# One matmul of 512 columns for the high weight half, with the parts added when a projection is drained

## Chip, cores and metric

One core of a Trainium2 chip runs one program that holds a whole small network. The metric is the device time of one execution in microseconds, lower is better; the median of several executions is compared. TensorE (PE) multiplies, ScalarE (ACT) and VectorE (DVE) work on the results and prepare operands, GpSimd (POOL) and SyncE (SP) only issue transfers here, apart from small things.

## What is computed

256 tokens of width 2048 pass through two blocks, in float32. The first has two layers, each an RMS norm, a wide input projection (`w_in`), three attention mixers behind it, an output projection (`w_o`), and a gated addition with a second projection:

```python
for i in range(DEPTH):
    u = rms_norm(h, norm_g[i])
    z = u @ w_in[i]
    ...
    h = h + mixed @ w_o[i]
    h = h + (p[i] @ w_ple[i]) * jax.nn.sigmoid(h @ w_pg[i])
```

The second block has four layers on `x` and on a context of 256 tokens: Fourier mixing, window attention, a gated depthwise convolution, Fourier mixing. Each begins with a modulated norm and ends with a gated addition, and shift, scale and gate come from a product of a condition vector with the modulation weights:

```python
shift, scale, gate = ada_modulation(c, ada_w[i], ada_b[i])   # silu(c) @ w + b, 2048 x 6144 a layer
h = rms_norm_2(x, norm_g[i]) * (1.0 + scale[:, None, :]) + shift[:, None, :]
...
x = x + gate[:, None, :] * o
```

## The kernel before

**Splits.** TensorE multiplies in fp32r, a reduced format. Full precision is kept by splitting each operand into a high and a low half: weights into `whi` (an ACT cast, L1092, the helper `split` on ACT) and `wlo` (a DVE subtraction, L1701, `split` on DVE), activations into `uhi` and `ulo`. A product is the sum of three: `whi`*`uhi` (L529), `whi`*`ulo` (L530), `wlo`*`uhi` (L533).

**Slabs and groups.** Weights stream from HBM in slabs of 128 x 2048 floats (1 MB), four buffers of them (`raw`, with `wlo` in the same place; `whi` has two). A group is four slabs (s = 0 to 3) and gives four blocks of 128 output channels x 256 tokens, which fill two PSUM banks. Slab s holds input tiles kt = 4s to 4s+3 for all four blocks, so `slab_t` issues 16 pairs L529/L530, and then 16 times L533. Groups take the bank pairs 0/1 and 2/3 in turn, so that a group's drain may last as long as the next group's four slabs. `stream_plan` lists the runs: `in0`, `in1` (the input projections), `ga` (gates), `ple`, `o`, `pg`, and in the second block `fci`, `fco`, `fxi`, `fxo`, `f3i`, `f3o` (Fourier in and out on context, x, and the last layer), `kvc`, `kvx`, `qz`, `ao` (attention), `ci`, `co` (convolution). Kind "T" are those that go through `slab_t`. In the before kernel that includes `ga`.

**Order.** On ACT and DVE every run is an order written by hand: `run` calls the splits, two slabs ahead of TensorE, the drain of group g-1 after the split of slab 1 of group g, hooks (squares and folds of the next norm), and on DVE `ada(r, pos)`. A drain either copies (`copier`, ACT), applies a function into a buffer (`gater`, ACT), or adds to the residual with a gate (`adder`, DVE).

**Modulation pieces.** The modulation product is not on TensorE: 384 pieces of 128 x 1024 floats (0.5 MB) are loaded by POOL (L473) into two buffers `aslab`, and each is one multiply-and-sum on DVE (L1726), or two for the first 160 pieces, which serve both conditions. `ada_due` says how many pieces are taken at each slab position of each run.

**Borders.** Where a run needs a norm of what the run before it made, the norm stands between them (`norm`: n0, n1, nci, nf3, end), or is made in chunks while the last group runs (`norm_chunks`: nfc, nfx, nkc, nx1). In `norm` the sum of squares goes over TensorE (L652), and then DVE and ACT make `uhi`/`ulo` tile by tile, and TensorE waits for each tile of slab 0. After tile 8 DVE puts the split of slab 1 in between.

Of the kernel before, what the change touches and what calls it, by code (L numbers as in the profile page):

```python
# [17 lines left out]
F32 = mybir.dt.float32  # L18
# [50 lines left out]
def stream_plan():  # L69
# [32 lines left out]
    m = a = e = 0  # L102
    for r in runs:
        r["m0"], r["a0"], r["e0"] = m, a, e
        m += r["n"]
        a += r["ada"]
        e += r["steps"]
# [7 lines left out]

def ada_due(r, pos):

    def upto(p):
        if r["name"] in ("in0", "in1"):
            return 30 * min(max(p - 3, 0), 25) // 25  # L120
        if r["name"] == "ci":
            return min(p, r["ada"])
        if r["name"] in ("ga0", "ga1", "pg1", "fco", "fxo"):
            return r["ada"] * min(p, 13) // 13
        if r["name"] == "fci":
            return 14 * min(p, 16) // 16 + max(0, p - 16)
# [6 lines left out]
        if r["name"] == "o1":  # L133
            return min(p, 3) + 10 * max(0, p - 7) // 9
# [22 lines left out]
TAIL_NORMS = ("n0", "n1", "nx1", "nci", "nf3", "end")  # L157
U_NORMS = {n: i for i, n in enumerate(n for n in FILLS if n[0] == "n")}
# [35 lines left out]
def build(nc, w, vec, out):  # L194
    ctx = ExitStack()
    with ctx:
# [20 lines left out]
        uhi_t = sb("uhi", KT * T, F32R)  # L217
        ulo_t = sb("ulo", KT * T, F32R)
# [80 lines left out]
        bank = [ctx.enter_context(nc.psum_tensor(f"bank{i}", [P, 512], F32)) for i in range(8)]  # L299
# [27 lines left out]
        s_drain = sem("projection_drained")  # L327
        s_gu = sem("gate_used")
# [50 lines left out]
        s_cg = sem("conv_gates_ready")  # L379
# [20 lines left out]
        def squares(name, c):  # L400
# [3 lines left out]
            return (sq[:, 0:1024], sq[:, 1024:2048], pt[:, :], sq[:, 1024:2048])[c]  # L404

# [61 lines left out]
        def _(pool):  # L467
# [30 lines left out]
            for i, b in enumerate(PE_BLOCKS):  # L498
# [3 lines left out]
                pool.wait_ge(s_drain, 2 * (RUN["ci"]["e0"] + b // 2 + 1))  # L502
# [10 lines left out]
        def _(pe):  # L513
# [11 lines left out]
            def step_banks(e):  # L525
                return (bank[2 * (e % 2)], bank[2 * (e % 2) + 1])
# [8 lines left out]
            def slab_t(s, par, lows, ready=None):  # L535
                for k in range(4):
                    kt = 4 * s + k
                    if ready is not None:
                        pe.wait_ge(*ready(kt))
# [59 lines left out]
            def group(r, g, par, slab, fill=None, after=None, middle=None):  # L599

                e = g + r["e0"]
                if not (isinstance(e, int) and e < 2):
                    pe.wait_ge(s_drain, (e - 1) * 2)
                for s in range(SLABS):
                    if fill in NORMS and slab is slab_t:
                        pe.wait_ge(s_hi, (g + r["m0"]) * SLABS + (s + 1))
                        slab(s, par, False, lambda kt: (s_nl, 16 * U_NORMS[fill] + kt + 1))
# [13 lines left out]
            def project(name, fill, g0=0, n=None, sums=()):  # L621
# [4 lines left out]
                if sums:  # L626
                    for g in range(g0, g0 + n):
# [4 lines left out]
                        group(r, g, (r["e0"] + g) % 2, slab, fill if g == g0 else None, behind)  # L632
                    return
                for g in range(g0, g0 + min(n, 2)):
                    group(r, g, (r["e0"] + g) % 2, slab, fill if g == g0 else None)
                if n > 2:
                    with pe.Fori(g0 // 2 + 1, (g0 + n) // 2) as j:
                        for half in range(2):
                            group(r, j * 2 + half, (r["e0"] + half) % 2, slab)
                    if n % 2:  # L640
                        group(r, g0 + n - 1, (r["e0"] + n - 1) % 2, slab)

            def norm(name):
# [6 lines left out]
                if tail:  # L650
                    pe.wait_ge(s_sf, 4 * n + 4)
                    last = nc.tensor.matmul(bank[7][:, 0:T], ones[:, :], squares(name, 3)[:, 0:T],  # L652
# [11 lines left out]
            def first_block(l):  # L664
# [34 lines left out]
                for g in range(3):  # L699
                    group(r, g, (r["e0"] + g) % 2,  # L700
# [90 lines left out]
                for g in range(4):  # L791
                    group(r, g, (r["e0"] + g) % 2, slab_t, None, lambda s, g=g: point(2 * (4 * g + s) + 1),
# [4 lines left out]
                for s in range(SLABS):  # L797
                    pe.wait_ge(s_drain, 2 * (r["e0"] + s - 1))
                    pe.wait_ge(s_lo, SLABS * r["m0"] + s + 1)
                    b0, b1 = step_banks(r["e0"] + s)  # L800
# [11 lines left out]
            def up(l, jobs):  # L812
# [12 lines left out]
                for b in range(15):  # L825
                    e = r["e0"] + b // 4
                    o = step_banks(e)[(b % 4) // 2][:, T * (b % 2):T * (b % 2) + T]
# [4 lines left out]
                    if b % 4 == 0:  # L832
                        pe.wait_ge(s_drain, 2 * (e - 1))
# [14 lines left out]
                for part, (s, c0, n) in enumerate(((2, 1024, 512), (3, 0, 256))):  # L848
                    e = r["e0"] + 4 + part
                    pe.wait_ge(s_drain, 2 * (e - 1))  # L850
                    need(s)
                    for t in range(2):
                        tk = slice(P * t, P * (t + 1))
                        o = step_banks(e)[t][:, 0:n]
# [10 lines left out]
            def fourier(tag, n_inv):  # L865
# [50 lines left out]
                for g in range(4, 8):  # L916
                    group(r, g, (r["e0"] + g) % 2, slab_t, None, lambda s, g=g: after(4 * (g - 4) + s))
# [22 lines left out]
            for g in range(4, 8):  # L940
                group(r, g, (r["e0"] + g) % 2, slab_t, None, lambda s, g=g: rope_behind(4 * (g - 4) + s))
            pe.wait_ge(s_ro, 2 * NJ + NJX)

            U0, T0 = 2 * N1, 2 * NT1
# [1780 lines left out]
```

## Time and profile before

| | us |
|---|---|
| runs before (3) | 3159.17 to 3162.21, median 3160.34 |
| the profiled execution | 3164.51 |
| its span, first to last instruction | 3162.8 |
| PE busy | 2995.5 (95%) |
| DVE busy | 2435.8 (77%) |
| ACT busy | 1364.2 (43%) |
| mean granted TensorE clock | 0.981 |

Busy time of an engine is time in which at least one of its instructions runs. Matmuls overlap in the records, so the distance between the starts of two of them, not the duration of one, says what a matmul costs in a stream. The three runs and the profiled execution lie within 0.17%.

### The profile page before, as it was taken

To read this page: it belongs to the slowest core of one execution; us is meant where nothing else is said; L and a number is where in the kernel's file an instruction comes from. 1 tells how busy PE (TensorE), PEld (TensorE's weight loads), DVE (VectorE), ACT (ScalarE), POOL (GpSimd) and SP (SyncE) were. 2 spreads that over 40 slices of the span, in tenths; PEclk is the share of its full clock that TensorE was granted. 3 is DMA by queue.
4 is the path that set the end of the run, shared out by engine and by line. 5 is a ranking of instruction groups with operands and counts; after the bars stand their busy time and mean duration, and the time that the engine had idled before them with its cause. 6 is when DMAs were issued, how large, how long until landed. Compare 5 with 4: busy or idle time off the path is not lost.

```text
span 3162.8 us, 57851 instructions
## 1 busy us (share of the span) xinstructions
PE 2995.5 (95%) x23922; PEld 2868.5 (91%) x23922; DVE 2435.8 (77%) x3378; ACT 1364.2 (43%) x1480; POOL 274.4 (9%) x530
## 2 busy tenths in 40 slices
PE   5999999989999999999999998999898999989998
PEld 5997889989978899899999998998698999889998
DVE  7877888888888889975875777677878976577465
ACT  4444553343444644443443444334734333534343
POOL 0100000101000000000000110100010422000000
PEclk9999999989999999999999999999999999999999
DMA  6875547758845487675767774865276765477563
GB/s 230 294 268 173 169 160 265 256 200 290 287 160 174 161 295 278 214 258 202 280 236 256 258 276 163 301 242 192 81 254 212 228 197 195 152 261 249 204 227 133
DMA packets 130956, 706.32 MB, mean 223 GB/s; under 512 B 16393, under 2 KB 16545, under 8 KB 72609
## 3 DMA queue, kind: packets, MB, share of 16 engines
q1 hardware_dynamic: 67392, 480.28, 43.5%
q0 software_dynamic: 61264, 214.93, 20.0%
q10 hardware_dynamic: 2064, 7.70, 0.7%
q8 instruction: 182, 2.98, 0.4%
q14 instruction: 54, 0.43, 0.0%
HBM read 696.07 MB, written 2.10 MB: 221 GB/s over the span
## 4 chain that ended last, share of the span: by engine, by line
PE 59%; DVE 11%; issue 3%; ACT 3%; DMA 2%; DVEq 0%; POOLq 0%; ACTq 0%
PE bank L533 18%; PE bank L529 16%; PE bank L530 16%; DVE wlo L1701 3%; DMA aslab<-w_ada_dram 2%; DVE aslab L1726 2%; ACT whi L1092 2%; PE bank L881 1%; DVE sc L1872 1%; PE bank L995 1%; DVE junk L1726 1%; PE bank L661 1%; PE bank L902 1%; PE bank L953 1%; DVE yc L2456 1%
## 5 line engine op out<-in xcount | busy, mean ns | idle before, releaser
L529 PE MATMUL bank<-uhi,whi 128*128 128x256 f32 x6656 | 1651.6, 288 | 54.2 <-ACT whi L1092 18.1
L530 PE MATMUL bank<-ulo,whi 128*128 128x256 f32 x6656 | 1635.0, 285 | 0.0
L1092 ACT CAST whi<-raw 128x2048 fp32r<-128x2048 f32 x456 | 861.1, 1890 | 1424.6 <-PE bank L533 1386.4
L1701 DVE TENSOR_TENSOR wlo<-raw,whi 128x2048 fp32r<-128x2048 f32 x456 | 1034.7, 2270 | 440.7 <-ACT whi L1092 440.1
L529 PEld LDWEIGHTS bank<-uhi,whi 128*128 128x128 f32 x6656 | 1293.3, 194 | 66.9 <-issue 48.2
L530 PEld LDWEIGHTS bank<-ulo,whi 128*128 128x128 f32 x6656 | 1293.3, 194 | 3.0 <-issue 2.4
L533 PE MATMUL bank<-uhi,wlo 128*128 128x256 f32 x6656 | 880.6, 285 | 22.9 <-DVE wlo L1701 22.8
L533 PEld LDWEIGHTS bank<-uhi,wlo 128*128 128x128 f32 x6656 | 834.7, 193 | 28.8 <-DVE wlo L1701 26.1
L473 POOL DMA_DIRECT2D aslab<-w_ada_dram x384 | 203.7, 531 | 2636.0 <-DVE mod L1726 1392.3
L1726 DVE CUSTOM_DVE_ANT_0 aslab<-aslab,sil,part 128x1024 f32<-128x1024 f32 x192 | 245.1, 1280 | 47.5 <-DMA aslab<-w_ada_dram 47.5
L1726 DVE CUSTOM_DVE_ANT_0 aslab<-aslab,sil,cols 128x1024 f32<-128x1024 f32 x192 | 245.3, 1280 | 46.5 <-DMA aslab<-w_ada_dram 46.5
L1726 DVE CUSTOM_DVE_ANT_0 junk<-aslab,sil,cols 128x1024 bf16<-128x1024 f32 x80 | 102.4, 1280 | 23.3 <-DMA aslab<-w_ada_dram 20.2
L1726 DVE CUSTOM_DVE_ANT_0 junk<-aslab,sil,part 128x1024 bf16<-128x1024 f32 x80 | 102.3, 1279 | 9.7 <-DMA aslab<-w_ada_dram 7.5
L2456 DVE SCALAR_TENSOR_TENSOR yc<-gp,cols,yc 128x256 f32<-128x256 f32 x240 | 97.4, 478 | 0.0
L533 PE MATMUL bank<-whi,ulo 128*128 128x512 f32 (+2 forms) x256 | 84.5, 344 | 0.0
L594 PE MATMUL bank<-whi,uhi 128*128 128x512 f32 (+1 forms) x192 | 72.7, 391 | 1.1 <-ACT whi L1092 1.1
L1387 ACT ACTIVATE sc<-sc,sm 128x128 f32<-128x128 f32 x84 | 37.6, 448 | 64.1 <-DVE sm L2153 63.9
L1601 ACT ACTIVATE xs<-xs,sm 128x513 f32<-128x513 f32 x64 | 45.8, 717 | 30.7 <-DVE sm L2396 30.7
L533 PEld LDWEIGHTS bank<-whi,ulo 128*128 128x128 f32 x256 | 50.2, 196 | 8.1 <-issue 3.4
L1235 ACT ACTIVATE uhi<-sc,mod 128x256 fp32r<-128x256 f32 x64 | 29.2, 504 | 60.5 <-DVE sc L1872 57.7
L533 PE MATMUL bank<-wlo,uhi 128*128 128x512 f32 (+2 forms) x256 | 53.6, 336 | 0.0
L2396 DVE CUSTOM_DVE_ANT_0 xs<-bank,k,lamr 128x512 f32<-128x512 f32 x64 | 45.5, 748 | 8.9 <-PE bank L953 8.7
(289 smaller groups left out, 2283.7 us busy)
## 6 DMA issues: line engine op xcount, KB each, us to landing
aslab<-w_ada_dram POOLq DMA_DIRECT2D x384, 512.0 KB, 5.2
raw<-w_wfi_dram SPq DMA_DIRECT2D x96, 1024.0 KB, 5.1
raw<-w_win_dram SPq DMA_DIRECT2D x88, 1024.0 KB, 5.2
raw<-w_wfo_dram SPq DMA_DIRECT2D x48, 1024.0 KB, 5.1
raw<-w_wci_dram SPq DMA_DIRECT2D x48, 1024.0 KB, 5.2
raw<-w_wo_dram SPq DMA_DIRECT2D x32, 1024.0 KB, 6.2
raw<-w_wpg_dram SPq DMA_DIRECT2D x32, 1024.0 KB, 5.5
raw<-w_wqz_dram SPq DMA_DIRECT2D x32, 1024.0 KB, 5.1
```

What stands on the lines that cost most here:

```text
L473: pool.dma_start(aslab[:, slot, :], w["ada"][i]).then_inc(s_araw[slot], 16)
L529: nc.tensor.matmul(o, w_, xhi_, start=start, stop=False, skip_group_check=True)
L530: nc.tensor.matmul(o, w_, xlo_, start=False, stop=False, skip_group_check=True)
L533: return nc.tensor.matmul(o, w_, xhi_, start=False, stop=stop, skip_group_check=True)
L594: nc.tensor.matmul(o, uhi[:, kt, tk], whi[:, s % 2, wc], start=kt == 0, stop=False, skip_group_check=True)
L1092: nc.scalar.copy(whi[:, s % 2, 0:n], raw[:, s, 0:n]).then_inc(s_hi, 1)
L1387: last = nc.scalar.activation(x, x, ACT.Exp, bias=sm[:, SM_NM + c:SM_NM + c + 1], scale=-1.0, accum_out=sm[:, SM_SUM + c:SM_SUM + c + 1])
L1601: nc.scalar.activation(x, x, ACT.Exp, bias=sm[:, SM_NM + c:SM_NM + c + 1], scale=-1.0, accum_out=sm[:, SM_SUM + c:SM_SUM + c + 1]).then_in ...
L1701: v.tensor_tensor(wlo[:, s, 0:n], raw[:, s, 0:n], whi[:, s % 2, 0:n].bitcast(F32), ALU.subtract).then_inc(s_lo, 1)
L1726: ins = v.tensor_tensor_reduce(out=junk[:, :] if c else x, in0=x, in1=sil[:, c if both else 1 - half, :], scale=1.0, scalar=col("ada_b_2", ...
L2396: v.tensor_tensor_reduce(out=xs[:, 2 * (t % 3) + odd, 0:512], in0=bank[odd][:, :], in1=mask2[:, b], scale=-0.125, scalar=nsink[:, h:h + 1] ...
L2456: ins = v.scalar_tensor_tensor(out=yc[:, b, :], in0=x, scalar=wt, in1=yc[:, b, :], op0=ALU.mult, op1=ALU.add)
```

## The change

In the projections of kind "T" (all but `ga`, which gets its own kind "G" and the old slab layout) the two matmuls with `whi` become one: `uhi` and `ulo` now lie in one tensor, and the moving operand is both of them, 2 x 256 columns. A block then needs a whole PSUM bank: `whi`*`uhi` and `wlo`*`uhi` in columns 0 to 255, `whi`*`ulo` in columns 256 to 511. The slabs are laid out anew on the host: slab s holds eight input tiles for two of the four blocks, slabs 0 and 2 for the first two blocks, slabs 1 and 3 for the other two. The bank pairs change with each slab, so the first half of a group is complete after slab 2, the second after slab 3, and each half must be drained before the same slab parity of the next group begins.

The drain adds the parts: ACT copies the second part to SBUF (`corr`), DVE adds it to the first (`onto_copy`, or `in_place` in PSUM, after which ACT applies its function, `post`); `adder` does two rounds from PSUM. Drains go by halves and stand before the split of slab 0 and of slab 1 of the next group. The last squares before a border go by halves too, and a filled chunk of activations is now awaited by slab pairs (`chunk_free`). The modulation pieces are given out anew.

```diff
-        run(f"in{l}", "T", "win", 11 * l, 7, ada=30)
+        run(f"in{l}", "T", "win", 7 * l, 7, ada=26)
-        run(f"ga{l}", "T", "win", 11 * l + 7, 4, ada=13)
+        run(f"ga{l}", "G", "wga", 4 * l, 4, ada=(8, 13)[l])
-        run(f"o{l}", "T", "wo", 4 * l, 4, ada=(17, 13)[l])
-        run(f"pg{l}", "T", "wpg", 4 * l, 4, ada=(18, 14)[l])
+        run(f"o{l}", "T", "wo", 4 * l, 4, ada=(16, 13)[l])
+        run(f"pg{l}", "T", "wpg", 4 * l, 4, ada=(12, 8)[l])
...
-            run("qz", "T", "wqz", 0, 8, ada=36)
+            run("qz", "T", "wqz", 0, 8, ada=50)
-            run("ao", "T", "wao", 0, 4, ada=18)
+            run("ao", "T", "wao", 0, 4, ada=20)
-            run("co", "T", "wco", 0, 4, ada=18)
-        run(which + "i", "T", "wfi", 8 * j, 8, ada={"fc": 30, "fx": 42, "f3": 32}[which])
-        run(which + "o", "T", "wfo", 4 * j, 4, ada=0 if which == "f3" else 12)
+            run("co", "T", "wco", 0, 4, ada=16)
+        run(which + "i", "T", "wfi", 8 * j, 8, ada={"fc": 28, "fx": 54, "f3": 32}[which])
+        run(which + "o", "T", "wfo", 4 * j, 4, ada={"fc": 12, "fx": 14, "f3": 0}[which])
...
         if r["name"] == "qz":
-            return 20 * min(p, 16) // 16 + max(0, p - 16)
+            return 26 * min(p, 16) // 16 + 24 * max(0, p - 16) // 16
         if r["name"] == "fxi":
-            return 18 * min(p, 16) // 16 + 24 * max(0, p - 16) // 16
+            return 24 * min(p, 16) // 16 + 30 * max(0, p - 16) // 16
...
             def slab_t(s, par, lows, ready=None):
+                for k in range(8):
+                    kt = 8 * (s // 2) + k
+                    if ready is not None and ready(kt) is not None:
+                        pe.wait_ge(*ready(kt))
+                    for b in range(2):
+                        wc = slice(2 * P * k + P * b, 2 * P * k + P * (b + 1))
+                        o = bank[2 * par + b]
+                        if lows:
+                            last = low(o[:, 0:T], wlo[:, s, wc], uhi[:, kt, :], kt == KT - 1)
+                        else:
+                            last = nc.tensor.matmul(two(o[:, :]), whi[:, s % 2, wc], both_u[:, :, kt, :],
+                                                    start=kt == 0, stop=False, skip_group_check=True)
+                return last
...
+            def copier(dest):
+                def corr(r, g, half):
+                    second_parts(r, g, half)
+                    nc.scalar.copy(two(dest(g, half)), rest_of(r, half)).then_inc(s_cq, 1)
+                return corr, no_corr
...
+            def in_place(r, g, half, x):
+                dve.wait_ge(s_cq, SUMMED[r["name"], g, half][0])
+                half_summed(r, g, half)
+                v.tensor_tensor(main_of(r, half), main_of(r, half), x, ALU.add).then_inc(s_add, 1)
+
+            def onto_copy(r, g, half, x):
+                dve.wait_ge(s_cq, SUMMED[r["name"], g, half][0])
+                half_summed(r, g, half)
+                v.tensor_tensor(x, main_of(r, half), x, ALU.add).then_inc(s_drain, 1)
...
+                def add(r, g, half):
+                    at = 1024 * g + 512 * half
+                    half_summed(r, g, half)
+                    for part in range(2):
+                        src = (rest_of, main_of)[part](r, half)
```

## Rows read from the trace of the kernel before

**Rows 1.** The page's chain of work that ended last, shares of the span.

```profile
PE 59%; DVE 11%; issue 3%; ACT 3%; DMA 2%; DVEq 0%; POOLq 0%; ACTq 0%
```

**Rows 2.** Stretches: us, busy PE, PEld, DVE, ACT, POOL (count), PEclk, DMA share, GB/s.

```profile
546.00:649.00 103.00, 97.11 (x773) 96.70 (x772) 91.84 (x104) 40.61 (x30) 10.07 (x19) 0.95 0.76 264
...
1190.00:1282.00 92.00, 91.92 (x766) 91.69 (x765) 88.81 (x99) 43.90 (x32) 8.48 (x16) 1.00 0.78 274
...
1500.00:1593.00 93.00, 93.00 (x776) 92.95 (x775) 72.05 (x73) 40.85 (x28) 9.01 (x17) 1.00 0.77 277
...
1960.00:2060.00 100.00, 96.96 (x794) 96.58 (x794) 69.89 (x76) 42.66 (x38) 11.13 (x21) 0.98 0.79 277
```

**Rows 3.** The chain within 1500 to 1593 us, and within 2374 to 2500 us.

```profile
by line: PE bank L533 33.5%; PE bank L530 33.0%; PE bank L529 33.0%; PE bank L648 0.5%
by line: DVE wlo L1701 16.8%; DVE yc L2456 16.0%; issue 10.1%; DVE aslab L1726 9.8%; PE bank L529 7.6%; PE bank L530 7.4%; PE bank L533 7.1%; DMA aslab<-w_ada_dram 6.2%; DVE sc L1872 5.1%; DVE ulo L1883 4.1%; PE bank L995 2.9%; ACT whi L109
```

**Rows 4.** Groups of matmuls by shape: count, busy us, mean ns, idle before.

```profile
L529 PE MATMUL bank<-uhi,whi 128*128 128x256 f32 x6656 | 1651.6, 288 | 54.2 <-ACT whi L1092 18.1 <-DVE ulo L1883 10.6 <-DVE ulo L1880 8.5
L533 PE MATMUL bank<-uhi,wlo 128*128 128x256 f32 x6656 | 880.6, 285 | 22.9 <-DVE wlo L1701 22.8
L594 PE MATMUL bank<-whi,uhi 128*128 128x512 f32 x128 | 55.8, 436 | 1.1 <-ACT whi L1092 1.1
```

**Rows 5.** Timeline: start us, us; every second matmul of two steady streams.

```profile
200.23 0.28 PE L529 MATMUL bank<-uhi,whi 128*128 128x256 f32 x1
...
200.47 0.28 PE L529 MATMUL bank<-uhi,whi 128*128 128x256 f32 x1
...
214.13 0.39 PE L594 MATMUL bank<-whi,uhi 128*128 128x512 f32 x1
...
215.04 0.39 PE L594 MATMUL bank<-whi,uhi 128*128 128x512 f32 x1
```

**Rows 6.** Groups of DVE and ACT that drain or split: count, busy us, mean ns.

```profile
L1825 DVE TENSOR_TENSOR h<-bank,h 128x512 f32<-128x512 f32 x16 | 10.2, 681 | 0.0
L1830 DVE SCALAR_TENSOR_TENSOR h<-bank,mod,h 128x256 f32<-128x256 f32 x64 | 26.5, 475 | 14.7 <-PE bank L533 14.7
L1092 ACT CAST whi<-raw 128x2048 fp32r<-128x2048 f32 x456 | 861.1, 1890 | 1424.6 <-PE bank L533 1386.4 <-PE bank L523 26.2 <-PE bank L861 4.9
L1160 ACT ACTIVATE zq<-bank 128x512 f32<-128x512 f32 x16 | 8.6, 592 | 9.6 <-PE bank L533 9.6
```

**Rows 7.** Waits of PE within 546 to 700 us: total, times, longest.

```profile
PE bank L533 <- DVE wlo L1701: 10.1, 3, 4.3
```

**Rows 8.** Timeline of the border from `ao` over the norm nci to `ci`.

```profile
2391.91 1.66 DVE L1830 SCALAR_TENSOR_TENSOR h<-bank,mod,h 128x256 f32<-128x256 f32 x4 [4.92 <-PE bank L533]
2393.65 1.06 ACT L1187 ACTIVATE sq<-h 128x1024 f32<-128x1024 f32 x1 [4.02 <-issue]
2394.74 0.69 DVE L1778 TENSOR_TENSOR sq<-sq 128x512 f32<-128x512 f32 x1 [1.17 <-ACT sq L1187]
...
2402.49 0.55 PE L529 MATMUL bank<-uhi,whi 128*128 128x256 f32 x1 [5.32 <-DVE ulo L1883]
...
2407.94 2.08 PE L533 MATMUL bank<-uhi,wlo 128*128 128x256 f32 x16
...
2409.60 0.48 DVE L1883 SCALAR_TENSOR_TENSOR ulo<-sc,mod,uhi 128x256 fp32r<-128x256 f32 x1
```

**Rows 9.** Timeline of DVE and POOL in `qz`: a split, pieces, a load, a late piece.

```profile
1989.23 2.29 DVE L1701 TENSOR_TENSOR wlo<-raw,whi 128x2048 fp32r<-128x2048 f32 x1 [3.46 <-ACT whi L1092]
1991.44 1.28 DVE L1726 CUSTOM_DVE_ANT_0 aslab<-aslab,sil,part 128x1024 f32<-128x1024 f32 x1
...
1992.65 1.28 DVE L1726 CUSTOM_DVE_ANT_0 aslab<-aslab,sil,part 128x1024 f32<-128x1024 f32 x1
...
2001.27 0.53 POOL L473 DMA_DIRECT2D aslab<-w_ada_dram  x1 [6.16 <-DVE mod L1726]
...
2005.46 1.28 DVE L1726 CUSTOM_DVE_ANT_0 aslab<-aslab,sil,cols 128x1024 f32<-128x1024 f32 x1 [3.57 <-DMA aslab<-w_ada_dram]
```

More of the change, by code:

```diff
@@ L1138, in run @@
-                if (n - 1) % 2:
-                    body(g0 + n - 1, (r["e0"] + g0 + n - 2) % 2, fill)
+                g = g0 + n - 1
+                following = then if then is not None else (early,)
+                nxt, g1 = following[0], following[1] if len(following) > 1 else 0
+                corr(r, g, 0)
+                if nxt is not None:
+                    split(RUN[nxt], g1, 0)
+                post(r, g, 0)
+                hook(g + 1, 0)
+                corr(r, g, 1)
+                if then is not None:
+                    split(RUN[nxt], g1, 1)
@@ L1140, in run @@
+                post(r, g, 1)
                 if fill is not None:
-                    split(RUN[then[0]], 0, 0)
                     fill(2)
-                    split(RUN[then[0]], 0, 1)
-                elif then is not None:
-                    presplit(*then)
-                if early is not None:
-                    split(RUN[early], 0, 0)
-                drain(r, g0 + n - 1, (r["e0"] + g0 + n - 1) % 2)
-                if fill is not None:
-                    fill(3)
-            def nothing(r, g, par):
-                pass
@@ L1155, in copier, with run_one @@
-            def copier(dest, func=ACT.Copy):
-                def drain(r, g, par):
-                    summed(r, g)
-                    for half in range(2):
-                        last = nc.scalar.activation(dest(g, half), bank[2 * par + half][:, :], func)
-                    last.then_inc(s_drain, 2)
-                return drain
-            def gater(first, func, g0):
-                def drain(r, g, par):
+                    fill(3)
+            def run_one(r, drain, then):
+                split(r, 0, 2)
+                split(r, 0, 3)
+                presplit(*then)
+                drain(r)
@@ L1734, in run @@
                 n = r["n"] if n is None else n
+                add, use = drain
                 def hook(g, s):
@@ new lines, in copier, with applier, add, gater @@
+            def copier(dest):
+                def add(r, g, half):
+                    onto_copy(r, g, half, two(dest(g, half)))
+                return add, no_step
+            def applier(dest):
+                def add(r, g, half):
+                    in_place(r, g, half, two(dest(g, half)))
+                return add, no_step
+            def gater(first, g0):
+                def dest(g, half):
+                    at = 1024 * ((first + g - g0) % 2) + 512 * half
+                    return sq[:, at:at + 512]
+                return applier(dest)
@@ new lines, in adder, with add @@
+            def adder(dest_t, gate):
+                def add(r, g, half):
+                    at = 1024 * g + 512 * half
+                    half_summed(r, g, half)
+                    for part in range(2):
+                        src = (rest_of, main_of)[part](r, half)
+                        if gate is None:
+                            last = v.tensor_tensor(two(dest_t[:, at:at + 512]), src, two(dest_t[:, at:at + 512]),
+                                                   ALU.add)
+                        else:
+                            for b in range(2):
+                                y = dest_t[:, at + T * b:at + T * (b + 1)]
+                                last = v.scalar_tensor_tensor(out=y, in0=src[:, b, :], scalar=gate(4 * g + 2 * half + b),
+                                                              in1=y, op0=ALU.mult, op1=ALU.add)
+                        if part == 0:
+                            link(last)
+                    last.then_inc(s_drain, 1)
+                return add, no_step
```

551 lines of the change are left out of this document (352 added, 199 removed).

## The prediction, made before the changed kernel ran

> **What bounds the kernel now.** I read the chain of work first: most of it is TensorE, then DVE [rows 1]. Cut into stages, the table of stretches shows TensorE busy without a break where a projection runs undisturbed (16 slabs of `fco` in 93 us, 776 matmuls, so 0.12 us each), with DVE at 77% [rows 2]. The chain inside that stretch is nothing but the three matmul lines in equal parts [rows 3]. The chain inside the first groups of `ci` looks different: splits, convolution taps and modulation pieces on DVE lead [rows 3]. In `pg0`, 103 us for 15 to 16 slabs, TensorE lost time, and the view of waits names the late `wlo`: 10.1 us in three waits [rows 2, 7]. So the bound is TensorE's issue pace in most of the span, DVE in a few stages, and latency at the borders between runs.
>
> **What a merged pair saves.** Two 256-column matmuls start 0.24 us apart as a pair, 200.23 to 200.47 [rows 5]. Four 512-column ones take 0.91 us, 214.13 to 215.04, or 0.2275 each, on the same 128 x 128 weights in the same format [rows 5]. The pair with `whi` (L529, L530) becomes one of 512 and saves 0.24 - 0.2275 = 0.0125 us. Groups of kind T after the change: in 14, o 8, pg 8, qz 8, ao 4, ci 12, co 4, Fourier in 24, Fourier out 12, together 94, or 376 slabs of 16 pairs = 6016 of the 6656 [rows 4]. Sum: 6016 x 0.0125 = **75.2 us**, 0.20 us a slab (5.76 becomes 5.56). The array still sees as many columns; only a fixed cost per matmul goes. 512 columns from two places, 256 each, are in no row. From below, the step could be worth nothing if two pieces cost what two matmuls cost; from above it is 0.0133 us, where only 256/2.4 GHz = 0.1067 of the 0.12 us is columns, so 80 us. I take the row.
>
> The Trainium skill, "TensorE: Matmul & The Clock Gate", section on the back-to-back issue gap, gives 262 cycles for 256 columns and 518 for 512, so a merged pair would save 6 cycles, 2.5 ns, and the change 15 us instead of 75. The rows of this kernel disagree with it (0.12 us is 288 cycles at 2.4 GHz, 0.2275 is 546), and they decide.
>
> **What the drains cost.** Per half group (2 blocks): on ACT a copy of 0.59 us, on DVE an add of 0.68 [rows 6]. ACT has room: each split takes 1.89 of 5.56 us [rows 6]. DVE gets 66 x 2 adds of 0.68, 8 groups of `o` with two more of 0.68, and 20 gated groups with four more of 0.475: 90 + 11 + 38 = 139 us, raising it from 77% to some 83% of a shorter span. That is 0.35 us a slab, which hides where DVE's slab sum (split 2.21, pieces 1.21 or, for two conditions, 2.42, by distance of starts [rows 9]) stays under 5.56. Worked out: `in0` 2.21 + 1.04 x 2.42 + 0.3 = 5.0; `o0` 88 us of 89; `fco` far below. If that cover were gone, the whole 139 us would show.
>
> The deadline moves too. Before, a drain could last four slabs. Now a half that is complete after slab 2 must be empty one slab later, 5.56 us. Its steps are copy 0.59 and add 0.68, so 1.3 us, and where ACT applies a function it does that after its next split: 0.59 + 1.89 + 0.59 = 3.1. Behind the waiting add on DVE stands the split of the next slab, due 5.56 + 3.64 (its 16 high matmuls) = 9.2 us after the same moment and done at 4.7, and behind that the pieces. Both fit. What shrinks is the lag that DVE may have before TensorE feels it: 5.56 - 1.3 = 4.3 us at a drain (3.7 with a function behind it), where the split before had 5.76 + 3.84 - 1.89 - 2.21 = 5.5.
>
> **The modulation pieces.** `pg0` had 18 pieces at 2.42: with splits, folds and gating 93 us against TensorE's 92, and waits showed. It now has 12: 83 against 89. I give back 9 of the 10.1 us [rows 7]. `pg1` goes from 14 to 8 pieces, while `fci` gets all its 28 at the double price, and its first half (85 us and 6 us of late chunk) stands at 91 against 89; I call these even. `ci`: pieces in its first three groups, with 28 taps a group, already make DVE lead [rows 3]; two adds and a multiply in place of one add 1.4 us in each of two groups: **+3**. `qz` gets 26 pieces in its first 16 slabs: 16 x 1.05 + 26 x 0.524 = 30.4 MB in 89 us = 342 GB/s. The stretch before had 277 GB/s at a DMA share of 0.79, so full share would be 350 [rows 2]. A piece took 4.2 us from issue to use and DVE waited 3.57 of it [rows 9]. With two buffers a piece can come each (0.5 + 4.2 + 1.2)/2 = 3.0 us at best, and one is wanted each 3.4. DVE has 17 us to wait in there, and will use it up. From nothing to 20 us, I take **+8** for `qz` and **+3** for `fxi` (24 in 16 slabs, 330 GB/s).
>
> **Borders.** The tail gets shorter: on 2391.91 follow four gated adds (1.66), a square of 1024 columns (1.06), and a fold of 512 (0.69) before the last fold [rows 8]. By halves the square is 0.6 and the 0.69 falls away: -1.15, five times: **-5.5**. The start gets longer: slab 0 now wants tiles 0 to 7, not 0 to 3. Tiles come each 0.79 us, and the split that DVE puts after tile 8 stands before the low half of tile 7, which the row shows at 2409.60 to 2410.08 [rows 8]. Slab 0's high part then ends at 2410.6 and slab 1 at 2418.1; before, slab 0's low part began at 2407.94 [rows 8], which puts the end of slab 1 at 2415.6. That is 2.4 later with the 0.4 saved already in it, so 2.8 each, at n0, n1, nci, nf3: **+11.2**. At nfc, nfx, nkc both first chunks (8 tiles, 6.3 us) now stand in front of the drain of the last group's first half, which so ends some 1.3 to 2.1 us after slab 3: **+5.1**. Before attention one step more on each engine: **+1**.
>
> **Sum.** -75.2 - 9 - 5.5 + 3 + 8 + 3 + 11.2 + 5.1 + 1 = -58.4. Of the profiled execution's 3164.5 (span 3162.8, 1.7 around it) that leaves 3106.1; the runs' median is 4.2 lower, 3160.3, and gives **3101.9**, -1.85%.
>
> **Rivals.**
> (a) The pace saving shows almost whole: DVE and DMA waits hide in lag, and the borders' losses are small because TensorE at 1.2 GHz after the gap is no faster than the tiles come. Then -75 - 9 - 5 + 10: 3081. For it: PE busy 93.00 of 93 with DVE waits inside. Against: the border arithmetic. Chance 0.17.
> (b) DVE becomes the bound in the stages with one and more pieces a slab. In `in0`, `in1`, `o0`, `fci`, `fxi`, `qz`, some 150 slabs, it would take back the 0.2 us of each, or 30 us beyond my terms: 3132. For it: DVE 88.81 of 92 in `pg1` [rows 2]. Against: TensorE did not stall there (91.92). Chance 0.15.
> (c) The merged matmul saves 2.5 ns, or two pieces cost as two. The sum is then -15 or 0 with +31 and -14.5: 3162 to 3177, no change or slower. The 2.5 ns is what the skill's page on TensorE gives. Rows 5 speak against the first; nothing but likeness against the second. Chance 0.05.
> (d) Slower: the half drain misses its deadline. It decides from 5.56 us after the half's last matmul; if each of 94 group starts waited 0.75 us (the drain at 6.3 us), 70 us would go and the time be 3172. It needs DVE to lag 4.4 to 5 us at every group start, while in the undisturbed stretch DVE idles a quarter of the time [rows 2]. Chance 0.03.
> My own case, 3087 to 3118: 0.60.
>
> **Numbers.** A measurement of this kernel tells 0.2% (6 us) from no change. Faster 0.92 (own case, a and b), same 0.04 and slower 0.04 (c and d). The range must take in (a) and most of (b): 3070 to 3138 leaves some 0.12 outside; my own case alone gives 3087 to 3118.
>
> **What would show it.** In the profile after: 17,906 matmuls; a new group of 512 columns, x6016, with starts 0.2275 us apart and slabs of 5.56 us in `fco`; if it reads 0.24, (c) is right. DVE busy near 2575 us, and ACT near 1440. PE waits for `wlo` near 546 to 640 us mostly gone, those in `qz`, `fxi` and early `ci` grown, with DVE waiting for the pieces; slab 0 after nci, nf3 with gaps between its high matmuls. Waits of PE at group starts on a drain would speak for (d). The prediction is wrong in kind if PE in `fco` is no longer busy throughout.

## The result, and the profile after

The changed kernel takes 3192.99 us (median of 6 runs, 3178.54 to 3200.28) where the kernel before takes 3159.8 (6 runs): a ratio of 1.0101, 95% interval 1.0086 to 1.0115. It is 33 us slower. The prediction, 3102 us, was wrong in sign, and the measured time lies 55 us above its range (3070 to 3138). The profiled execution took 3195.91 us, its span is 3194.3, and the mean granted clock is 0.968.

From the page after: busy times, chain of work, and the costliest groups.

```profile
PE 2953.2 (92%) x17906; PEld 2562.2 (80%) x17906; DVE 2566.8 (80%) x3622; ACT 1404.8 (44%) x1560; POOL 272.9 (9%) x530
...
PE 63%; DVE 17%; DMA 10%; issue 6%; ACT 4%; POOLq 0%; ACTq 0%; DVEq 0%
...
L622 PE MATMUL pair<-u,whi 128*128 128x512 f32 x6016 | 1497.5, 402 | 129.9 <-DVE zf L2014 19.0
...
L1884 DVE CUSTOM_DVE_ANT_0 aslab<-aslab,sil,part 128x1024 f32<-128x1024 f32 x192 | 245.0, 1280 | 63.7 <-DMA aslab<-w_ada_dram 63.7
L1884 DVE CUSTOM_DVE_ANT_0 aslab<-aslab,sil,cols 128x1024 f32<-128x1024 f32 x192 | 245.0, 1280 | 60.6 <-DMA aslab<-w_ada_dram 60.5
```

The counts are as forecast (17,906 matmuls, 6016 of 512 columns, DVE busy 2567 us, ACT 1405). What is new is in the chain: DMA stands at 10%, all of it `aslab<-w_ada_dram`, the modulation pieces, where it was 2% [rows 1]. The idle time in front of the high matmuls is 129.9 us, against 54.2 before [rows 4].

The stretches after (columns as in [rows 2]), each cut from the first weight load of a stage to that of the next, a few slabs ahead of its matmuls: `pg0`, `pg1`, `fco`, `fxi`, `qz`, `ao`. The last one has the attention in front of `ao` in it.

```profile
543.60:633.50 89.90, 89.35 (x514) 78.78 (x513) 86.12 (x96) 43.91 (x35) 7.39 (x14) 1.00 0.75 268
1177.40:1266.40 89.00, 89.00 (x513) 78.68 (x512) 76.65 (x80) 45.83 (x37) 4.09 (x8) 1.00 0.66 236
1489.20:1584.70 95.50, 91.64 (x515) 80.33 (x515) 89.08 (x105) 42.02 (x30) 8.96 (x17) 0.98 0.75 269
1584.70:1808.40 223.70, 205.94 (x1158) 180.17 (x1158) 161.68 (x209) 86.86 (x95) 23.22 (x44) 0.96 0.71 253
1973.20:2188.90 215.70, 197.34 (x1093) 170.48 (x1092) 162.49 (x185) 80.94 (x70) 24.26 (x46) 0.94 0.75 266
2188.90:2420.00 231.10, 198.38 (x1537) 160.83 (x1536) 184.49 (x404) 119.00 (x219) 22.18 (x42) 0.94 0.48 169
```

In `pg1` everything is as forecast: 16 slabs in 89.00 us without a gap, 5.56 each, where before they took 92.6. `pg0` came down from 102.7 to 89.9. Then it goes wrong. Before, the same cuts gave 92.6 us for `fco`, 211.2 for `fxi`, 197.8 for `qz` and 216.7 for `ao`: the four are 48 us longer now, and TensorE's clock in the last three is 0.96, 0.94 and 0.94, where it was 1.00, 0.99 and 0.97.

What happens there is in the timeline of `fxi` (start us, us, engine and line; in brackets the idle time before it and what ended it). Most of what lies in between is left out:

```profile
1620.46 0.53 POOL L549 DMA_DIRECT2D aslab<-w_ada_dram  x1 [40.63 <-DVE part L1884]
...
1621.65 0.53 POOL L549 DMA_DIRECT2D aslab<-w_ada_dram  x1 [0.66 <-DVE part L1884]
...
1624.64 1.28 DVE L1884 CUSTOM_DVE_ANT_0 aslab<-aslab,sil,cols 128x1024 f32<-128x1024 f32 x1 [3.64 <-DMA aslab<-w_ada_dram]
...
1625.85 2.29 DVE L1859 TENSOR_TENSOR wlo<-raw,whi 128x2048 fp32r<-128x2048 f32 x1
...
1630.20 1.28 DVE L1884 CUSTOM_DVE_ANT_0 aslab<-aslab,sil,cols 128x1024 f32<-128x1024 f32 x1 [2.06 <-DMA aslab<-w_ada_dram]
1631.14 0.58 ACT L1276 COPY zf<-pair 128x512 f32<-128x512 f32 x1 [4.19 <-PE pair L609]
...
1631.43 1.28 DVE L1884 CUSTOM_DVE_ANT_0 aslab<-aslab,sil,cols 128x1024 f32<-128x1024 f32 x1
...
1632.14 0.53 POOL L549 DMA_DIRECT2D aslab<-w_ada_dram  x1 [5.02 <-DVE part L1884]
...
1637.64 1.28 DVE L1884 CUSTOM_DVE_ANT_0 aslab<-aslab,sil,cols 128x1024 f32<-128x1024 f32 x1 [4.91 <-DMA aslab<-w_ada_dram]
...
1638.85 0.69 DVE L2014 TENSOR_TENSOR zf<-pair,zf 128x512 f32<-128x512 f32 x1
...
1639.60 5.45 PE L622 MATMUL pair<-u,whi 128*128 128x512 f32 x16 [8.49 <-DVE zf L2014]
```

Read it from the end. TensorE waited 8.49 us for an add of 0.69 us. ACT had copied the second part by 1631.72, so the add could have run when DVE was done with the piece of 1631.43, at 1632.7. It stands in DVE's order behind one more modulation piece, and DVE waited 4.91 us for that piece's data. The load of a piece is issued only when a buffer is free, that is when an earlier piece has been used. The pieces used at 1624.64, 1630.20 and 1637.64 were issued at 1620.46, 1621.65 and 1632.14, so 4.2, 8.5 and 5.5 us before their use. The granted clock (third column from the end) in the same place:

```profile
1624.00:1628.00 4.00, 1.81 (x8) 1.15 (x7) 3.36 (x3) 2.93 (x3) 0.53 (x1) 1.00 0.87 308
1628.00:1632.00 4.00, 2.92 (x16) 2.62 (x16) 1.94 (x4) 0.85 (x2) 0.00 (x0) 0.66 0.55 203
1632.00:1640.00 8.00, 0.41 (x1) 0.41 (x2) 3.09 (x6) 1.53 (x1) 1.47 (x3) 0.50 0.71 262
1640.00:1644.00 4.00, 4.00 (x13) 3.12 (x13) 4.00 (x5) 0.00 (x0) 0.51 (x2) 0.63 0.39 131
1644.00:1650.00 6.00, 6.00 (x36) 5.28 (x35) 5.24 (x6) 1.92 (x1) 1.18 (x3) 1.00 0.57 173
```

TensorE waits for `wlo` until 1628.19, and then for the add; the clock falls to half, 1.2 GHz, and it is still there when TensorE has work again: its 16 matmuls at 1639.60 take 5.45 us, where the 16 at 1621.99, at full clock, took 3.81. The DMA share there is 0.39 to 0.87, so the DMA engines had time left. How much of a load's 4.2 to 8.5 us is its own latency and how much the traffic beside it, these rows don't tell. The Trainium skill, "TensorE: Matmul & The Clock Gate", Part 1, says that the throttled state is the default and that activity releases it; these rows agree, with 0.50 where TensorE waited and 1.00 from 1644 us on.

TensorE's waits for drains after (total us, times, longest). None of them has a counterpart among the waits before; with the smaller ones they make 85 us. The row of `sm` is no drain but the start of the attention, where the longest wait is 10.6 us and was 2.6 before:

```profile
PE pair L622 <- DVE zf L2014: 19.0, 5, 8.5
PE pair L622 <- DVE zq L2014: 14.3, 4, 5.5
...
PE pair L622 <- DVE h L2040: 12.9, 3, 6.3
PE pair L1053 <- DVE sm L2629: 12.3, 2, 10.6
...
PE pair L622 <- ACT sq L1285: 10.6, 3, 6.8
PE pair L622 <- DVE h L2045: 9.9, 4, 4.5
```

L2014 is the add of `onto_copy`, L2040 and L2045 are those of `adder`, L1285 is the function behind an add in place.

To weigh the experiments I cut every profile into its 27 stages, as in the table of stretches, and summed two columns: time in which TensorE is idle, and time lost to the clock. The clock loss is (1 - clock) x TensorE's busy time, summed over stretches of 2 us, so that a low clock while TensorE is idle is not counted twice. The rest is called work. The sums leave out the last norm, and each kernel has one profiled execution.

| kernel | stages, us | work | idle | clock loss |
|---|---|---|---|---|
| before | 3155.9 | 2954 | 160 | 42 |
| after | 3187.3 | 2888 | 234 | 66 |
| e1_old_plan | 3146.3 | 2889 | 203 | 55 |
| e2_new_plan | 3189.9 | 2957 | 191 | 42 |
| e3_adds_first | 3161.6 | 2895 | 220 | 47 |
| e4_small_loads | 3136.0 | 2885 | 196 | 55 |
| e5_unmerged | 3195.9 | 2957 | 190 | 49 |
| e6_thin_adds | 3120.8 | 2889 | 189 | 43 |
| e7_order_old_plan | 3137.5 | 2895 | 194 | 49 |
| e8_order_mixed_plan | 3150.9 | 2894 | 213 | 45 |
| e9_before_small | 3142.7 | 2951 | 153 | 39 |
| e10_old_plan_small | 3130.2 | 2889 | 192 | 49 |

The work is 2951 to 2957 us in the four kernels with two matmuls a pair, and 2885 to 2895 in the eight with one, so these sums are good to some 5 us.

### The profile page after: what moved, and what is told of

It is laid out like the page before. It is cut to its first block, busy times and chain, and to the rows that moved or that the text cites. A ratio compares the mean times of both kernels' runs of the same rounds, so it can differ in the third digit from the quotient of the medians.

```text
span 3194.3 us, 46355 instructions
## 1 busy us (share of the span) xinstructions
PE 2953.2 (92%) x17906; PEld 2562.2 (80%) x17906; DVE 2566.8 (80%) x3622; ACT 1404.8 (44%) x1560; POOL 272.9 (9%) x530
## 4 chain that ended last, share of the span: by engine, by line
PE 63%; DVE 17%; DMA 10%; issue 6%; ACT 4%; POOLq 0%; ACTq 0%; DVEq 0%
PE pair L622 29%; PE pair L609 19%; DMA aslab<-w_ada_dram 10%; DVE wlo L1859 4%; DVE aslab L1884 4%; ACT whi L1202 2%; PE pair L605 2%; PE pair L606 2%; DVE sc L2086 1%; PE pair L683 1%; DVE junk L1884 1%; PE bank L980 1%; PE bank L761 1%; PE bank L1095 1%; DVE u L2097 1%
## 5 line engine op out<-in xcount | busy, mean ns | idle before, releaser
L622 PE MATMUL pair<-u,whi 128*128 128x512 f32 x6016 | 1497.5, 402 | 129.9 <-DVE zf L2014 19.0
L622 PEld LDWEIGHTS pair<-u,whi 128*128 128x128 f32 x6016 | 1138.0, 194 | 379.2 <-issue 50.5
L609 PEld LDWEIGHTS pair<-u,wlo 128*128 128x128 f32 x6656 | 853.5, 191 | 40.3 <-DVE wlo L1859 8.6
L609 PE MATMUL pair<-u,wlo 128*128 128x256 f32 x6656 | 873.0, 283 | 6.1 <-DVE wlo L1859 6.1
L605 PE MATMUL pair<-u,whi 128*128 128x256 f32 x640 | 162.1, 291 | 9.1 <-ACT whi L1202 3.4
L606 PE MATMUL pair<-u,whi 128*128 128x256 f32 x640 | 158.4, 285 | 0.0
L605 PEld LDWEIGHTS pair<-u,whi 128*128 128x128 f32 x640 | 124.5, 195 | 10.7 <-issue 4.2
L606 PEld LDWEIGHTS pair<-u,whi 128*128 128x128 f32 x640 | 124.6, 195 | 0.1
L609 PE MATMUL pair<-whi,u 128*128 128x512 f32 (+2 forms) x256 | 84.5, 343 | 0.0
L1276 ACT COPY sq<-pair 128x512 f32<-128x512 f32 x40 | 23.4, 585 | 116.3 <-PE pair L609 116.3
L683 PE MATMUL pair<-whi,u 128*128 128x512 f32 (+1 forms) x192 | 72.6, 390 | 0.0
L2045 DVE SCALAR_TENSOR_TENSOR h<-pair,mod,h 128x256 f32<-128x256 f32 x128 | 56.0, 479 | 11.1 <-PE pair L609 9.4
```

Of the source, the lines that this page charges most:

```text
L605: nc.tensor.matmul(o, w_, xhi_, start=start, stop=False, skip_group_check=True)
L606: nc.tensor.matmul(o, w_, xlo_, start=False, stop=False, skip_group_check=True)
L609: return nc.tensor.matmul(o, w_, xhi_, start=False, stop=stop, skip_group_check=True)
L622: last = nc.tensor.matmul(two(o[:, :]), whi[:, s % 2, wc], both_u[:, :, kt, :], start=kt == 0, stop=False, skip_group_check=True)
L683: nc.tensor.matmul(o, uhi[:, kt, tk], whi[:, s % 2, wc], start=kt == 0, stop=False, skip_group_check=True)
L2045: last = v.scalar_tensor_tensor(out=y, in0=src[:, b, :], scalar=gate(4 * g + 2 * half + b), in1=y, op0=ALU.mult, op1=ALU.add)
```

## Experiments

Every ratio is to the kernel before, run on the same chip beside the kernel.

### The two halves of the change apart: e1 and e2

e1_old_plan is the changed kernel with the piece plan of before (counts, positions, and the places of the `silu` hooks). e2_new_plan is the kernel before with the new plan. For e1, against the changed kernel:

```diff
-            run("qz", "T", "wqz", 0, 8, ada=50)
+            run("qz", "T", "wqz", 0, 8, ada=36)
-        run(which + "i", "T", "wfi", 8 * j, 8, ada={"fc": 28, "fx": 54, "f3": 32}[which])
+        run(which + "i", "T", "wfi", 8 * j, 8, ada={"fc": 30, "fx": 42, "f3": 32}[which])
-            return 26 * min(p, 16) // 16 + 24 * max(0, p - 16) // 16
+            return 20 * min(p, 16) // 16 + max(0, p - 16)
```

> The changed kernel with the piece counts and positions of the kernel before (fxi 42, qz 36, pg0 18, pg1 14) and the condition loads where they were. Theory A, pieces that come late push DVE past the new one-slab deadline of a half drain: fxi, fxo, qz and ao lose some 40 us of their stalls, pg0 gets back its 10, so 3150 to 3170 us against 3193. Theory B, the merged matmul or the added drain work itself costs the time wherever it stands: no change, 3185 to 3200. Theory C, the piece plan alone is at fault: below 3130.

> The kernel before with the new piece plan alone. Theory A: the loose drain deadline of four slabs absorbs the late pieces, so 3145 to 3165 us (pg0 gains 10, something is lost in qz). Theory C, the plan alone is at fault: 3180 to 3200.

Measured: e1 3153.14 us (10 runs), ratio 0.9981 (0.9971 to 0.9992); e2 3197.04 us (4 runs), ratio 1.0129 (1.0099 to 1.016). 0.9981 x 1.0129 = 1.0110, and the whole change has 1.0101: the halves add. The plan alone costs 38 to 41 us, on either kernel, and the merged matmul with its drains gains only 6. So e1 came out by its theory A, but e2 by theory C: a drain that may last four slabs does not absorb the new plan's late pieces. They reach TensorE by another way there: DVE waits 172 us for pieces instead of 122, and TensorE waits 40.1 us for `wlo` instead of 22.8:

```profile
PE bank L533 <- DVE wlo L1701: 22.8, 15, 4.3
```
```profile
PE bank L535 <- DVE wlo L1701: 40.1, 29, 4.3
```

(The first row is of the kernel before, the second of e2.) In e1 the idle time is still 43 us above before, and TensorE waits 64 us at drains, which the kernel before did not wait for:

```profile
PE pair L620 <- ACT sq L1283: 23.8, 11, 7.4
...
PE pair L620 <- DVE h L2040: 11.2, 4, 6.8
PE pair L620 <- DVE h L2045: 7.7, 2, 3.9
```

### Where the plan's cost lies: e3 and e4

e3_adds_first is the changed kernel with every piece that stood directly in front of an add put behind it; e4_small_loads loads an eighth of each piece from 162 on.

```diff
                 for g in range(g0 + 1, g0 + n):
                     add(r, g - 1, 0)
+                    ada(r, 4 * g - 1)
                     split(r, g, 0)
                     use(r, g - 1, 0)
                     hook(g, 0)
-                    ada(r, 4 * g)
                     add(r, g - 1, 1)
+                    ada(r, 4 * g)
                     split(r, g, 1)
```
```diff
-                pool.dma_start(aslab[:, slot, :], w["ada"][i]).then_inc(s_araw[slot], 16)
+                pool.dma_start(aslab[:, slot, 0:n], w["ada"][i, :, 0:n]).then_inc(s_araw[slot], 16)
...
-                            out=junk[:, :] if c else x, in0=x,
+                            out=junk[:, :] if c or i > 161 else x, in0=x,
```

> The changed kernel with the modulation pieces that stood on DVE right before an add of parts put right behind it; same work, same counts. Theory A: TensorE's waits on the adds in fxi, qz and fxo shrink to a third and 15 to 35 us come back, 3158 to 3178. Theory B: no change beyond the scatter.

> The changed kernel with only 128 of 1024 columns of each piece loaded from piece 162 on (the modulations of the second block are then not those of the reference; DVE does the same multiplies, its products go to a scratch tile). Theory A: nothing waits for a piece from fco on, and 50 to 80 us come back, 3115 to 3145. Theory B: under 10 us.

Measured: e3 3176.19 us (4 runs), 1.0057 (1.004 to 1.0074), so 14 us of the change's 33 are order alone. That is the upper end of theory A's range, and the waits tell why it was not more. At drains they fall from 85 to 13 us. But the pieces now stand in front of the splits, and TensorE waits for `wlo` instead (first the changed kernel, then e3):

```profile
PE pair L609 <- DVE wlo L1859: 6.1, 4, 2.4
```
```profile
PE pair L609 <- DVE wlo L1859: 50.6, 30, 5.6
```

e4 3143.75 us (4 runs), 0.9944 (0.9927 to 0.9961), 49 us below the changed kernel with the same number of DVE instructions; theory A wanted 50 to 80, and B under 10. DVE's waits for pieces fall from 146 to 54 us. In `fxi` and `qz` it shows directly:

```profile
1584.20:1797.50 213.30, 204.51 (x1157) 179.21 (x1156) 163.23 (x210) 86.74 (x95) 23.63 (x44) 0.98 0.49 172
1951.10:2149.30 198.20, 192.02 (x1095) 167.10 (x1094) 164.82 (x186) 80.49 (x69) 24.71 (x46) 0.97 0.52 185
```

DVE is as busy as in the changed kernel (163 and 165 us), yet the stages are 10.4 and 17.5 us shorter. It is the wait for the load, not the product, that costs. The lighter traffic could also have helped the weight slabs, but these were in time anyway: after the first slab of all, ACT waits 4.3 us for slabs in the changed kernel and 4.3 in e4.

### Do the loads cost the other kernels too: e9 and e10

The same small loads in the kernel before, and in e1.

> The kernel before, in which pieces from 162 on load only 128 of their 1024 columns and put their products into a scratch buffer (their results are left out); the number of DVE instructions stays. Theory P (late pieces cost only where they stand in front of an add that TensorE needs within a slab, or where the new plan crowds them): the kernel before had no such add and its own plan, and gains little from small loads, 0 to 12 us. Rival Q (the 28 us of DVE waiting on pieces, and the traffic itself, always cost): the gain is 25 us or more, as in the changed kernel (49).

> The merged kernel with the old plan and the same small loads from piece 162 on. Theory P: the drains wait less on DVE, gain 10 to 25 us against 3153, so 3128 to 3143. Rival Q: as in the changed kernel, 40 us or more, 3105 to 3113. If neither gains over 5 us, the late pieces of the old plan never mattered, and the drains' cost of 43 us of idle is DVE's own time and order.

Measured on one chip: e9 3147.57 us (6 runs), 0.9947 (0.993 to 0.9965); e10 3138.63 us (4 runs), 0.9931 (0.9912 to 0.995). With the old plan the loads cost 0.5% with the merged matmul (0.9981 to 0.9931, 16 us) and 0.5% without it (17 us). So neither theory holds as I wrote it. The merged kernel's 16 us lie in P's range and far from Q's, but the kernel before gained more than P's 12 us, and the merged one no more than it. The tight drains do not make late loads dearer; the new plan does: its loads cost 49 us where those of the old one cost 16 (by the intervals, each good to some 7 us). Without their full loads the two plans differ by 0.9944 - 0.9931, 4 us, which the intervals don't tell from nothing. Of the plan's 38 us, some 33 go away with the size of the loads.

### What the matmul and the drains are worth: e5 and e6

e5_unmerged is e1 with the merged matmul issued as two of 256 columns, all else the same. e6_thin_adds is e1 with the DVE adds cut to 8 of 256 columns a block.

```diff
-                            last = nc.tensor.matmul(two(o[:, :]), whi[:, s % 2, wc], both_u[:, :, kt, :],
-                                                    start=kt == 0, stop=False, skip_group_check=True)
+                            nc.tensor.matmul(o[:, 0:T], whi[:, s % 2, wc], uhi[:, kt, :],
+                                             start=kt == 0, stop=False, skip_group_check=True)
+                            last = nc.tensor.matmul(o[:, T:2 * T], whi[:, s % 2, wc], ulo[:, kt, :],
+                                                    start=False, stop=False, skip_group_check=True)
```
```diff
-                v.tensor_tensor(x, main_of(r, half), x, ALU.add).then_inc(s_drain, 1)
+                v.tensor_tensor(x[:, :, 0:8], main_of(r, half)[:, :, 0:8], x[:, :, 0:8], ALU.add).then_inc(s_drain, 1)
```

> The first experiment (changed kernel, old piece plan, 3153 us) with the one matmul of 512 columns issued as two of 256 into the same bank columns; layout, drains and waits as they are. Theory D, the merge is worth its 12.5 ns on each of 6016 pairs and the half drains with their deadline took it back: 75 us slower less what the longer slab gives back in slack, so 3195 to 3228. Theory E, the merged matmul itself is worth little: 3153 to 3170.

> The first experiment with the DVE adds of parts cut to 8 of 256 columns a block (the whi*ulo part is left out of most results); the waits and their order stay. Theory D1, DVE's added time (some 130 us) makes the drains late: the 43 us of TensorE's idle time over the kernel before shrink by half or more and some clock comes back, 3110 to 3130. Theory D2, the form of the wait does it, whatever DVE's load: 3145 to 3155.

Measured: e5 3203.0 us (4 runs), 1.0136 (1.0119 to 1.0153). Merging is worth 1.0136 to 0.9981, 49 us (good to 6 by the intervals); theory D has its range, though the merge gave 49 and not 75. Work falls by 68 us (2957 to 2889), 11.3 ns for each of 6016; idle time (13) and clock loss (6) take 19 back. The stretch `fco` of e5, with every row of it as before the change ([rows 2]: no idle time, 0.12 us a matmul), is the first of these rows, its counterpart in e1 the second:

```profile
1519.80:1612.40 92.60, 92.60 (x772) 92.55 (x771) 78.13 (x87) 41.93 (x30) 8.98 (x17) 1.00 0.79 278
```
```profile
1502.60:1592.10 89.50, 89.50 (x516) 79.06 (x514) 78.27 (x87) 42.05 (x30) 8.97 (x17) 1.00 0.79 288
```

e6: 3124.8 us (4 runs), 0.9887 (0.9871 to 0.9904), 30 us below e1 by the ratios (0.94%). DVE's busy time falls from 2564 to 2470 us, so 94 us of adds cost 30 us of time. The time lies in D1's range, but D1 wanted the 43 us of added idle time halved, and they shrank by 14; another 12 us came from the clock. The waits at drains only went from 64 to 54 us. The idle time is still 189 us against 160.

### Better versions: e7 and e8

e7_order_old_plan is e1 with the order of e3, and with the split that stands between the tiles of a norm moved from tile 8 to behind tile 9, so behind the tiles that slab 0 now wants. e8_order_mixed_plan has the same order, and a plan between the two (`pg0` 12, `pg1` 8, `fxi` 50, `qz` 46, `attn2` 20).

```diff
-                    if kt == 8:
+                    if kt == 9:
                         split(RUN[AFTER_NORM[name]], 0, 1)
```

> The first experiment with the pieces put behind the adds, and in the norm at a border the split of slab 1 put after tile 9 instead of tile 8, so that TensorE has the low half of tile 7 before it. If the deadline is what costs: drain waits of 48 us halve, 3120 to 3140; the later split gives 2 us at each of four borders. If only DVE's sum counts: 3145 to 3153.

> The third experiment (new plan, adds first, 3176 us) with the later split at the borders and a plan between the two: o1's pieces placed as before, fxi 50, qz 46, attention 20, fci 30, fco 14, co 20. If the number of pieces per slab in fxi and qz sets the loss: 3140 to 3160; if the loss is not theirs: 3170.

Measured: e7 3145.64 us (5 runs), 0.996 (0.9945 to 0.9974): the fastest of those that leave nothing out, 13 us faster than the kernel before and 44 us faster than the change. Its gain over e1 is 7 us, and the two intervals just overlap. It missed its range of 3120 to 3140 and lies in that of the other case, where only DVE's sum counts. The drain waits did more than halve, 64 to 13 us, but as in e3 they came back in front of `wlo` (e1, then e7):

```profile
PE pair L607 <- DVE wlo L1859: 3.5, 2, 1.8
```
```profile
PE pair L607 <- DVE wlo L1859: 47.8, 32, 4.6
```

So little of the cost was the drain's deadline as such: DVE is late, and its lateness reaches TensorE through whichever of its results is due next. The later split at the borders did what was expected of it (at nci 23.5 us from the last matmul of `ao` to the end of slab 1, and 26.2 in e1): the waits for `uhi`/`ulo` fall by 7 us, those for drains and `wlo` together by 6. No run has the two edits apart.

e8 3153.66 us (10 runs), 0.9986 (0.9973 to 1.0), within its first range. In its profile `pg0` has 89.0 us, 16 less than e7, but `fco`, `fxi`, `qz` and `ao` together have 36 more: relief in the two `pg` stages is real, and costs more where its pieces go. I ran no plan that keeps the relief and finds room for the 12 pieces; whether there is one stays open.

## Why the prediction was wrong

Two steps failed. The plan of the pieces was priced at +5 us and cost 38, and the 139 us of adds on DVE with the one-slab deadline were priced at nothing and cost some 30. A third term, the merged matmul, was the right mechanism but yielded 49 us of 75. By the prediction's own parts, each measured by a pair of kernels (a difference of two ratios, good to some 6 us):

| part | predicted | measured | pair |
|---|---|---|---|
| merged matmul | -75 | -49 | e5 to e1 |
| drains, layout, borders | +12 | +43 | before to e5 |
| modulation pieces | +5 | +38 | e1 to after |
| sum | -58 | +32 | |

The +3 of `ci` stood with the pieces in the prediction and is counted there. The pairs before to e5 and e5 to e1 have the old plan of pieces.

**The pace: right, its yield was not.** The term 6016 x 0.0125 rested on [rows 5], and undisturbed stretches give it: 5.56 us a slab in `pg1`, and 3.1 us less for the 16 slabs of `fco`. 512 columns from two places cost what 512 in a row cost, which was the open point. The work fell by 68 us in the pair e5 to e1. The runs show 11 ns a pair, and the rows of `fco` 12. By the back-to-back gap of the Trainium skill, "TensorE: Matmul & The Clock Gate", 2.5 ns, the work would fall by 15 us; the trace disagrees. Rival (c) falls. But 19 us of the 68 came back as idle time and low clock: TensorE waits 64 us at drains in e1 and 51 in e5, with the same DVE work, since a faster TensorE is at each of them sooner. The prediction counted DVE's 5.0 of 5.56 us a slab as hidden, and had this loss only as rival (b).

**The drains' 139 us were not hidden.** "0.35 us a slab, which hides where DVE's slab sum (...) stays under 5.56." The sum was a mean, and DVE does its work in an order: e6 shows 30 us for the adds' time. Rival (b) had 30 us too, by another sum (150 slabs x 0.2 us), so the agreement is partly luck; its mechanism, DVE as the bound in the full stages, should have been in the forecast rather than beside it. `pg0` under the old plan shows the kind of stage: DVE has 99 of 107 us, and TensorE waits for the function behind an add (`sq`, 11.0 us in four waits), not for `wlo` as in [rows 7].

```profile
PE pair L620 <- ACT sq L1283: 11.0, 4, 7.4
PE pair L620 <- DVE h L2040: 1.9, 1, 1.9
PE pair L607 <- DVE wlo L1859: 1.7, 1, 1.7
```

**The deadline.** "Both fit" was worked out for a DVE that is on time. I worked out that DVE may lag 4.3 us at a drain (3.7 with a function), and put the chance of missing it at 0.03, because rival (d) was written as a miss at every one of 94 groups. It takes few: five waits for `zf` make 19.0 us and three for `h` 12.9. Lag comes in lumps: one late piece is 4.9 us, more than the whole allowance. How much the deadline costs by itself stays open. From before to e5 TensorE's waits at drains go from 0 to 51 us, but those for `wlo` fall from 22.8 to 5.1 and those for `whi` from 19 to 7, so much of it is the same lateness, met one step earlier. With the adds' time taken out (e6), 29 us of idle time above before are left, with the borders and the faster matmul's part in it.

**The borders** were priced well where I looked. At nci the time from the last matmul of `ao` to the end of slab 1's low part is 24.7 us after (2436.5 to 2461.2) against 23.9 before (2391.7 to 2415.6): +0.8 where my terms -1.15, +2.8 and -0.4 make +1.25. Over all borders TensorE's waits for `uhi`/`ulo` rise from 31.6 to 48.8 us (before to e5), and those for sums of squares fall from 54.0 to 47.9, near the -5.5. I had no term for the border before `co`, where slab 0 now wants two chunks of the convolution's output: TensorE waits 11.37 us there in e1 (part of the 48.8 in e5 too), and waited 7.2 us before, on nothing that the profile shows. By these waits the borders took some 4 us, less than their +12, and most of the +43 in the table is the drains'.

```profile
2736.08 6.64 PE L620 MATMUL pair<-u,whi 128*128 128x512 f32 x16 [11.37 <-DVE u L2144]
```

**The modulation pieces were the largest error.** The gain at `pg0` was given as 9 us, on top of 3 for the pace, and `pg0` is 12.8 us shorter than before, so that term held. `pg1` and `fci` were called even, and were: 9 us less and 8 more than in e1. But `qz` had +8 and became 18 us longer than in e1, `fxi` had +3 and got 14, and `fxo` (14 pieces), the attention with `ao` (20), `o1` and `fco` had nothing and got 12, 11, 8.5 and 6. The step that failed is "DVE has 17 us to wait in there, and will use it up". It compared a rate (a piece each 3.0 us at best, one wanted each 3.4) with a total of slack. The rate was wrong: the 4.2 us in it came from a single row. Over the first half of `qz` a load takes 5.6 us from issue to landing in the median (5.2 before), and (0.5 + 5.6 + 1.2)/2 = 3.65 us a piece is slower than the 3.4 wanted: by the prediction's own sum there was no slack to use up.

```profile
aslab<-w_ada_dram POOLq DMA_DIRECT2D x23, 512.0 KB, 5.6
```

And a total of slack is not what TensorE feels: it feels the wait that stands in front of the next add or split in DVE's order. DVE's total wait for pieces rose from 122 to 146 us, and the chain of work went from 2% to 10% on their loads. `o1` has 13 pieces in both plans; evenly over its slabs it takes 90.8 us, and in e1, with three early and ten late, 82.3. e8 has the places of e1 there, and 82.3 us again. It needs no more pieces to lose time; their places are enough.

**The clock had no term.** Every gap was priced at its length. The clock loss rose by 24 us from before to after, a third of the rise in idle time (74 us). The plan's own part: on the kernel before the idle time rises by 31 us and the clock loss by nothing, on e1 the idle time by 31 and the clock loss by 11. Why the same idle time costs the merged kernel more clock I did not settle.

My bounds for the drains and the plan ended at +20 us for `qz` and at zero for the rest; that is what made the range too narrow. Rivals (b) and (d) each described a part of what happened, and I treated them as alternatives.

## What to carry to other kernels

Price added work on an engine with hand-written order by its place: ask what stands between it and the consumer that is due next, and whether anything in front of it waits for a transfer. With two buffers a load starts only when an earlier piece has been used, so take its time from issue to landing as the median of the stage and not from one row, and check that rate before counting slack. Put an instruction that waits for data behind those that TensorE waits for, but expect it to delay what then stands behind it: here it took 72 us of drain waits away in e3 and 51 in e7, and gave 14 and 7 us of time, as 44 us of waits moved to the splits. Price a plan by its longest single wait against the tightest deadline. A change that speeds the bounding engine also moves every deadline forward, so expect part of the gain back as waits (19 us of 68 here), and add the low clock after each gap.

## What the runs showed of the hardware

One matmul of 512 columns that reads two pieces of 256, 256 x 16 = 4096 columns apart, starts each 0.228 us like one that reads 512 in a row: a slab of 5.56 us less 16 x 0.12 leaves 3.64 us for 16. At the low clock 14 of them took 5.38 to 5.86 us at the border nci, with the wait for tiles in it. Loads of an eighth of the size (64 KB) still took 3.4 us from issue to landing in `fxi`, against 5.1 us for the 512 KB in the changed kernel:

```profile
aslab<-w_ada_dram POOLq DMA_DIRECT2D x44, 64.0 KB, 3.4
```
```profile
aslab<-w_ada_dram POOLq DMA_DIRECT2D x44, 512.0 KB, 5.1
```

So two thirds of the time are left at an eighth of the size and with less traffic beside it. An estimate from these two: eight pieces of 64 KB would wait for some 27 us of loads where one of 512 KB waits for 5.1. That was not run. A third buffer was not tried either: it takes 4096 bytes a partition, and the kernel's tiles leave 344 below the limit that it asserts (229368). Separate parts added well: the product of two ratios (1.0110) gave the whole (1.0101) within the intervals, though each half reaches into the same order of instructions on DVE.
